# Five pairs of expert weight blocks are multiplied in plain fp32 instead of as a split pair; the ring of raw weight buffers is lengthened by four once

## The reference, cut to what matters

```python
top_vals, top_idx = lax.top_k(logits, TOP_K)
gates = ...                                  # softmax of the two, spread over 8 experts
for e in range(N_EXPERTS):
    out = out + gates[:, e:e + 1] * swiglu(t, w_gate[e], w_up[e], w_down[e])
# swiglu(t, g, u, d) = (silu(t @ g) * (t @ u)) @ d ;  g, u: 1024 x 1792, d: 1792 x 1024, all float32
```

## Time and profile before

| | us |
|---|---|
| median of 3 runs | 1148.93 (1148.74 to 1149.09) |
| the profiled execution | 1148.72 |
| its span in the profile | 1147.0 |
| PE busy | 1123.6 (98% of the span) |
| DVE busy | 875.3 (76%) |
| ACT busy | 754.1 (66%) |

### The profile page before, as it was taken

One profiled execution on the slowest core, in us unless ns is written; L12 is line 12 of the kernel. 1 busy time (PEld: TensorE's weight loads), 2 busy tenths in 40 slices (PEclk: granted clock), 3 DMA queues, 4 the chain that ended last, 5 costly groups with the idle time before them and its releaser, 6 DMA issues.

```text
span 1147.0 us, 15735 instructions
## 1 busy us (share of the span) xinstructions
PE 1123.6 (98%) x5566; PEld 946.4 (83%) x5566; DVE 875.3 (76%) x983; ACT 754.1 (66%) x941; POOL 35.1 (3%) x64
## 2 busy tenths in 40 slices
PE   9999999999999999999999999999999999999996
PEld 8888888888888888888888888887778887888874
DVE  6568676765554556468676779999999899999997
ACT  6555656455344345556656466799987898988785
POOL 3001000000000001001001000000000000000000
PEclk9999999999999999999999999999999999999999
DMA  9845533668555354646533657999999999999993
GB/s 322 278 141 183 175 99 98 210 207 311 183 181 187 110 173 144 217 133 186 172 101 125 198 178 249 405 396 406 407 407 394 371 398 403 405 407 406 407 384 128
DMA packets 120554, 294.96 MB, mean 257 GB/s; under 512 B 9006, under 2 KB 33676, under 8 KB 119964
## 3 DMA queue, kind: packets, MB, share of 16 engines
q1 hardware_dynamic: 119072, 288.23, 69.7%
q0 software_dynamic: 960, 5.28, 1.2%
q10 hardware_dynamic: 444, 0.47, 0.1%
HBM read 292.90 MB, written 1.05 MB: 256 GB/s over the span
## 4 chain that ended last, share of the span: by engine, by line
PE 79%; DVE 15%; DMA 3%; ACT 2%; issue 1%; SPq 0%; ACTq 0%; DVEq 0%
PE bank L1716 22%; PE bank L1717 21%; PE bank L1718 21%; DVE w_lo L1491 9%; DVE w_lo_more L1491 3%; PE bank L2130 2%; PE bank L2131 2%; PE bank L1932 2%; PE bank L1952 2%; PE bank L1760 2%; DMA raw<-in_moe_w_gate 1%; PE bank L1940 1%; DMA raw<-in_moe_w_down 1%; PE bank L2113 1%; ACT w_hi L941 1%
## 5 line engine op out<-in xcount | busy, mean ns | idle before, releaser
L1162 DVE TENSOR_TENSOR w_lo<-raw,w_hi 128x1024 fp32r<-128x1024 f32 (+4 forms) x141 | 240.1, 1708 | 144.2 <-ACT w_hi L721 143.7
L721 ACT ACTIVATE w_hi<-raw 128x1024 fp32r<-128x1024 f32 (+5 forms) x141 | 201.4, 1432 | 152.8 <-PE bank L1718 152.8
L1491 DVE TENSOR_TENSOR w_lo<-raw,w_hi 128x1792 fp32r<-128x1792 f32 (+3 forms) x148 | 287.2, 1971 | 10.8 <-ACT w_hi L941 10.0
L941 ACT ACTIVATE w_hi<-raw 128x1792 fp32r<-128x1792 f32 (+3 forms) x148 | 244.4, 1668 | 45.8 <-PE bank L1718 29.4
L1716 PE MATMUL bank<-w_hi,aT_hi 128*128 128x512 f32 (+1 forms) x592 | 235.1, 397 | 0.9 <-DVE aT_lo L1274 0.6
L1718 PE MATMUL bank<-w_hi,aT_lo 128*128 128x512 f32 (+1 forms) x592 | 230.0, 388 | 0.0
L1717 PE MATMUL bank<-w_lo,aT_hi 128*128 128x512 f32 (+1 forms) x592 | 229.5, 388 | 0.0
L1716 PEld LDWEIGHTS bank<-w_hi,aT_hi 128*128 128x128 f32 x592 | 111.3, 188 | 22.6 <-DVE w_lo L1284 1.4
L1718 PEld LDWEIGHTS bank<-w_hi,aT_lo 128*128 128x128 f32 x592 | 111.1, 188 | 22.8
L1717 PEld LDWEIGHTS bank<-w_lo,aT_hi 128*128 128x128 f32 x592 | 111.4, 188 | 20.3
L1491 DVE TENSOR_TENSOR w_lo_more<-raw,w_hi_more 128x1792 fp32r<-128x1792 f32 (+3 forms) x50 | 97.0, 1947 | 5.7 <-ACT w_hi_more L941 5.7
(11 more groups left out here) (326 smaller groups left out, 1806.6 us busy)
## 6 DMA issues: line engine op xcount, KB each, us to landing
raw<-in_moe_w_gate SPq DMA_DIRECT2D x128, 448.0 KB, 7.0
raw<-in_moe_w_up SPq DMA_DIRECT2D x128, 448.0 KB, 7.0
raw<-in_moe_w_down SPq DMA_DIRECT2D x112, 512.0 KB, 7.2
raw<-in_w_in SPq DMA_DIRECT2D x40, 768.0 KB, 4.5
raw<-in_dense_w_gate SPq DMA_DIRECT2D x22, 512.0 KB, 3.9
raw<-in_dense_w_up SPq DMA_DIRECT2D x22, 512.0 KB, 4.8
raw<-in_dense_w_down SPq DMA_DIRECT2D x11, 1024.0 KB, 4.9
raw<-in_w_in SPq DMA_DIRECT2D x20, 512.0 KB, 5.0
```

Of the source, the lines that this page charges most:

```text
L721: act.activation(dst, src, ACT.Copy).then_inc(hi_made[j], 1)
L941: act.activation(split_of(hi_slot, m), raw_of(i, n), ACT.Copy).then_inc(e_hi_made, 1)
L1162: dve.tensor_tensor(dst, src, high, ALU.subtract).then_inc(lo_made[j], 1)
L1491: dve.tensor_tensor(split_of(lo_slot, m), raw_of(i, n), split_of(hi_slot, m).bitcast(F32), ALU.subtract).then_inc(e_lo_made, 1)
```

## The change

In each even small step (k = 2, 4, 8, 10, 14) the pair of up granules n = 9 and 10 is no longer split. PE multiplies the raw float32 weights by the float32 view of the tokens, one matmul where there were two (the hi and the lo columns of the stationary operand stay as they are). ACT and DVE skip that pair. SP, before it loads into a raw slot that held such a granule, waits until PE has used it instead of until DVE has made its lo part. These pairs are granules 48 and 49, 94 and 95, 186 and 187, 232 and 233, 324 and 325.

Granules 52 to 55 (end of step 2) are loaded once into four other buffers, in `mixed` and `xs`, where the outputs of the first two experts come later. The ring of 12 raw slots goes on behind them as if they weren't there: granules 56 to 67 take over slots from 16 granules back instead of 12; from granule 68 on it is 12 again. ACT waits for DVE to have read these buffers before it writes the first outputs there. The final residual's buffers move with the ring (`H_SLOTS`).

```diff
+WHOLE = {SPLIT_OF[SEQ[r, k, KC + 2]] for r in range(ROUNDS) for k in SMALL_STEPS if k % 2 == 0}
...
+OUTSIDE = range(52, 56)
+
+def raw_slot_of(i):
+
+    if i in OUTSIDE:
+        return RAW_SLOTS + i - OUTSIDE[0]
+    return (i - (len(OUTSIDE) if i > OUTSIDE[-1] else 0) + RAW_SLOTS // 2) % RAW_SLOTS
...
-H_SLOTS = (2, 3, 4, 5)
+H_SLOTS = (10, 11, 0, 1)
...
 # SP, before each load
+                            if i in OUTSIDE:
+                                sp.wait_ge(logits_made, 1)
+                                sp.wait_ge(sq_act, 4)
+                                sp.wait_ge(sq_dve, 4)
+                            elif RAW_BEFORE[i] is None:
...
-                                sp.wait_ge(e_lo_made, SPLIT_OF[RAW_BEFORE[i]] + 1)
+                                if is_whole(RAW_BEFORE[i]):
+                                    sp.wait_ge(e_used, RAW_BEFORE[i] + 1)
+                                else:
+                                    sp.wait_ge(e_lo_made, splits_made(RAW_BEFORE[i]))
...
 # ACT and DVE
-                for m in sorted({SPLIT_OF[first], SPLIT_OF[first + 1]}):
+                for m in sorted({SPLIT_OF[first], SPLIT_OF[first + 1]} - WHOLE):
...
 # ACT, output_hi
+                if r == 0 and e < 2:
+                    act.wait_ge(e_lo_made, splits_made(OUTSIDE[2 * e + 1]))
...
 # PE, gate_up_granule
-                pe.wait_ge(e_lo_made, SPLIT_OF[i] + 1)
+                if is_whole(i):
+                    pe.wait_ge(*raw_arrival(i))
+                    for u in range(2):
+                        last = pe.matmul(bank[(B_GATE, B_UP)[n // KC][u]][:, 0:HN], xT[:, c, small_both(p, k % 4 // 2)].bitcast(F32),
+                                         raw_of(i)[:, 0, u * HN:(u + 1) * HN], start=c == 0, stop=c == KC - 1)
+                    last.then_inc(e_used, 1)
+                    return
+                pe.wait_ge(e_lo_made, splits_made(i))
```

More of the change, by code:

```diff
@@ L166, with is_whole, splits_made @@
 SPLIT_OF = {i + x: m for m, (i, n) in enumerate(SPLITS) for x in range(n)}
+WHOLE = {SPLIT_OF[SEQ[r, k, KC + 2]] for r in range(ROUNDS) for k in SMALL_STEPS if k % 2 == 0}
+MADE, made = [], 0
+for m in range(len(SPLITS)):
+    made += m not in WHOLE
+    MADE.append(made)
+def is_whole(i):
+    return SPLIT_OF[i] in WHOLE
+def splits_made(i):
+    return MADE[SPLIT_OF[i]]
 def slot_history(slots):
     return [i - slots if i >= slots else None for i in range(len(GRANULES))]
-H_SLOTS = (2, 3, 4, 5)
-def h_slots_read(r, slots):
-    return SPLIT_OF[max(i for i in range(PER_ROUND * r, PER_ROUND * (r + 1)) if (i + RAW_SLOTS // 2) % RAW_SLOTS in slots)] + 1
-RAW_BEFORE, W_BEFORE = slot_history(RAW_SLOTS), slot_history(W_SLOTS)
+OUTSIDE = range(52, 56)
[4 more added lines that the diff above has]
+H_SLOTS = (10, 11, 0, 1)
+def h_slots_read(r, slots):
+    return splits_made(max(i for i in range(PER_ROUND * r, PER_ROUND * (r + 1)) if raw_slot_of(i) in slots))
+W_BEFORE = slot_history(W_SLOTS)
+RAW_BEFORE, RAW_TURN, last_in = [], [], {}
+for i in range(len(GRANULES)):
+    RAW_BEFORE.append(last_in.get(raw_slot_of(i)))
+    RAW_TURN.append(1 if RAW_BEFORE[i] is None else RAW_TURN[RAW_BEFORE[i]] + 1)
+    last_in[raw_slot_of(i)] = i
 BETWEEN = {(STEPS - 1, 20): ("hidden", STEPS - 1, 0)}
@@ L239, in build_trunk @@
             [("raw", [P, 2, 3, SLOT])],
-            [("raw_pad", [P, H_SLOTS[0], SLOT_W]), ("h_hi", [P, NT, D], F32R), ("h_lo", [P, NT, D], F32R)])
+            [("raw_pad", [P, H_SLOTS[0], SLOT_W]), ("h_hi", [P, NT, D], F32R)],
+            [("h_lo", [P, NT, D], F32R)])
         w_hi = place("w_hi", [P, 3, SLOT], F32R)
@@ L354, in build_trunk @@
                              "x_hi_in", "x_lo_in", "selT_tr", "selT_in", "y_hi_made", "y_lo_made", "back_made"))
-        e_raw_in = [sem(f"e_raw_in{s}") for s in range(RAW_SLOTS)]
+        e_raw_in = [sem(f"e_raw_in{s}") for s in range(RAW_SLOTS + 1)]
         e_hi_made, e_lo_made, e_used, e_silu_made, e_hid_made, e_hid_tr, e_hT_hi_made, e_hT_lo_made = (sem(n) for n in (
@@ L442, in raw_of, with raw_arrival @@
         def raw_of(i, n=1):
-            at_slot = (i + RAW_SLOTS // 2) % RAW_SLOTS
-            return raw_slot[:, at_slot:at_slot + n, 0:granule_width(GRANULES[i][2])]
+            of, at_slot = raw_slot, raw_slot_of(i)
+            if i in OUTSIDE:
+                of, at_slot = (mixed, xs)[(i - OUTSIDE[0]) // 2], (i - OUTSIDE[0]) % 2
+            return of[:, at_slot:at_slot + n, 0:granule_width(GRANULES[i][2])]
+        def raw_arrival(i):
+            if i in OUTSIDE:
+                return e_raw_in[RAW_SLOTS], 16 * len(OUTSIDE)
+            return e_raw_in[raw_slot_of(i)], 16 * RAW_TURN[i]
         def split_of(slots, m):
@@ L610, in expert_loads @@
                                     experts_at[k // 2] = sp.value_load(order[0:1, at_rank:at_rank + 1], min_val=0, max_val=EXPERTS - 1)
-                            if RAW_BEFORE[i] is None:
-                                s = (i + RAW_SLOTS // 2) % RAW_SLOTS
+                            if i in OUTSIDE:
+                                sp.wait_ge(logits_made, 1)
+                                sp.wait_ge(sq_act, 4)
+                                sp.wait_ge(sq_dve, 4)
+                            elif RAW_BEFORE[i] is None:
+                                s = raw_slot_of(i)
                                 sp.wait_ge(lo_made[s % 6 // 2], MIX[1] + (BLK_MIX, BLK_MIX + 1)[s < RAW_SLOTS // 2] + 1)
                             else:
-                                sp.wait_ge(e_lo_made, SPLIT_OF[RAW_BEFORE[i]] + 1)
+                                if is_whole(RAW_BEFORE[i]):
+                                    sp.wait_ge(e_used, RAW_BEFORE[i] + 1)
+                                else:
+                                    sp.wait_ge(e_lo_made, splits_made(RAW_BEFORE[i]))
                             if n < GU_N:
@@ L621, in expert_loads @@
                                 src = moe_w_down[0][ds(experts_at[(k - 1) // 2], 1), row:row + P, :]
-                            sp.dma_start(raw_of(i)[:, 0, :], src.rearrange("o p n -> (o p) n")).then_inc(e_raw_in[i % RAW_SLOTS], 16)
+                            sp.dma_start(raw_of(i)[:, 0, :], src.rearrange("o p n -> (o p) n")).then_inc(raw_arrival(i)[0], 16)
                     expert_loads(0)
@@ L931, in expert_hi @@
             def expert_hi(first):
-                for m in sorted({SPLIT_OF[first], SPLIT_OF[first + 1]}):
+                for m in sorted({SPLIT_OF[first], SPLIT_OF[first + 1]} - WHOLE):
                     i, n = SPLITS[m]
                     for x in range(i, i + n):
-                        act.wait_ge(e_raw_in[x % RAW_SLOTS], 16 * (x // RAW_SLOTS + 1))
+                        act.wait_ge(*raw_arrival(x))
                     if W_BEFORE[i] is None:
@@ L1487, in expert_lo @@
             def expert_lo(first):
-                for m in sorted({SPLIT_OF[first], SPLIT_OF[first + 1]}):
+                for m in sorted({SPLIT_OF[first], SPLIT_OF[first + 1]} - WHOLE):
                     i, n = SPLITS[m]
-                    dve.wait_ge(e_hi_made, m + 1)
+                    dve.wait_ge(e_hi_made, MADE[m])
                     dve.tensor_tensor(split_of(lo_slot, m), raw_of(i, n), split_of(hi_slot, m).bitcast(F32),
```

## The result

The changed kernel takes 1155.36 us (median of 6 runs, 1154.45 to 1156.73) against 1148.84 us for the kernel before in the same sessions: a ratio of 1.0058, 95% interval 1.0048 to 1.0068, or 6.5 us slower. The forecast was 1153.8 us, slower by 5.1, with a range of 1148.5 to 1157.5; the measured time is inside it, 1.6 us above the forecast.

The account below looks back on a forecast made before the run. PE and DVE were taken to bound alternate stretches, with loads close behind. Steps 2, 4, 8, 10 and 14 added 1.4 + 0 + 0.9 + 1.4 + 1.4 = 5.1 us to 1148.72: 1153.8 us, range 1148.5 to 1157.5.

Parts of the forecast that it names:

- PE's price of an unsplit pair: PE's added work for each unsplit pair of granules: 1.44 us, 7.2 us over five pairs.
- rival 3: An unsplit matmul takes only the 0.41 us of the two it replaces, so PE pays nothing: 1144.2 us, chance 0.03.
- Steps 2, 10 and 14: PE's time is added in 2 and 14; in 10 the late silu leaves DVE idle: +1.4 us each.
- Step 8: PE's time is added, less about 0.5 us of its wait for a hidden lo part: +0.9 us.
- Step 4: Where DVE leads, PE's delay and DVE's relief cancel: 0, bounds -2.0 and +1.4 us.
- DVE's relief: Lo parts no longer made, 2.02 us a pair: hidden in PE's stretches, turned into idle wait in step 10.
- Rivals 1, 2: DVE's relief counts: in steps 4 and 10, 1148.4 us, chance 0.10; in step 14 too, 1145.0 us, chance 0.11.
- Rival 5: PE's gaps soak up the shift of steps 2 and 8, leaving 2.8 us: 1151.5 us, chance 0.12.
- SP's new wait: Raw slots of unsplit granules held until PE's use, longest in step 14: 0 on the path, other end +3 us.
- The four extra slots: Four loads go early, but PE leads there: 0, bound -1.1 us.
- rival 4: Loads starve as well; DMA idling of steps 10 and 14 lands on the path: +3, 1156.8 us, chance 0.12.

Follow-up runs that it names:

- experiment 3: Changed kernel with all pairs split, old SP waits; PE repeats the ten granules' products on 400 of 448 columns: 1153.52 us, 1.0043 against the kernel before.
- Experiment 5: Changed kernel, pairs multiplied from old hi and lo slots in PE's old time, ACT and DVE skipping them: 1151.79 us; also without SP's wait for PE: 1148.78.
- experiment 6: Changed kernel with the unsplit pair moved behind the gate rows' addition: 1156.62 us; the same move made to experiment 3: 1152.76 us.
- experiment 4: Changed kernel with all pairs split, SP still waiting for PE's use: 1151.34 us; holding only step 10's pair 1150.00, only step 14's 1149.76.

## Why the prediction was right

- **PE's price of an unsplit pair**, from attention's fp32 product: forecast 1.44 us, measured 1.37. Right. A matmul of 448 columns takes 2 x 0.376 = 0.75 us against 0.205 for one fp32r product, 3.7 times. That agrees with the four passes on the Trainium skill's page FP8 and Floating Point Precision, section TensorE Precision Notes. The half rate of rival 3, read as the cost of the whole matmul, would have given 0.41 and is excluded; each of the two records runs at nearly half rate.
- **Steps 2, 10 and 14**: +1.4, +1.45 and +1.4 in the chain, as forecast. Other traces with longer pairs agree: the kernel without extra slots and that of experiment 3 have +1.3 and +1.4 in step 10 and +1.4 and +1.45 in step 14.
- **Step 8**: +0.9, the right number with another cause. The forecast took 0.5 off because DVE's skipped work would shorten PE's wait for a hidden lo part. Experiment 3 skips nothing, and its trace shifts by 0.94 in the same place (901.94 to 903.61, 937.63 to 940.24); there too PE no longer waits for `hT_lo_buf`. PE itself comes later.
- **Step 4**: open. The chain shows 0.0 by the landmark at 824, but +0.8 by 852.34 (854.54), and the kernel without extra slots shows +1.3 and +1.05. The kernel with the slots alone gains 0.8 by 852 as well, with nothing changed in step 4. The forecast's balance of delay and relief has no support, as the relief alone measures nothing.
- **DVE's relief counts for nothing in the sum**: right, and more firmly so than argued. The forecast had it swallowed by the late silu in step 10, and let it cancel PE's delay in step 4. Experiment 5 shows it at 0, to within 1 us, even when no silu is late, and the traces of experiment 6 that the silu is one of two gates. Rivals 1, 2 and 3 are all out, and rival 3 by a second reason: with PE's cost and the held slots taken away the kernel stands at 1148.8, not 1144.2. Rival 5 is out as well: the shift of step 2 is not soaked up by PE's gaps (1.39 at 770, 1.40 at 824), nor is that of step 8.
- **The sum of PE's steps is right in part by luck.** The unsplit pairs add 5 x 1.37 = 6.9 us of PE work. Experiment 3 adds 7.3 us and measures +5.0. The forecast took a similar 2.1 us off, 7.2 to 5.1, but mostly on the strength of DVE's relief in steps 4 and 8, and experiment 3 has no relief. Its trace gives up the difference in step 4, in step 8 and behind step 14, where its shift falls by 1.2 us.
- **The step that was mis-sized is SP's new wait.** The forecast took it as 0 "on the path, since ACT reaches these granules late as well" and kept +3 as the other end. Alone, with the extra slots in the kernel, it measures +2.8 (1.0013 to 1.0031, 1.5 to 3.6 us), +2.1 against the slots alone. The reason given does not quite hold at the granules themselves, where ACT waits 0.29 us for the late load, and it left out what comes behind them: experiment 4 has loads on the chain 20 to 40 us later, where DVE has caught up with them. How the cost divides among the five steps is open: +1.2 for step 10 and +1.0 for step 14 both hold the slots' own +0.7.
- **The four extra slots**: 0, as forecast, within an interval of about 1 us each way.
- **The sum.** PE's time (+5.0) and held slots (+2.8) make 7.8, or 7.1 with the slots' +0.7 counted once; the whole change is 6.5. With intervals of about 1 us each way, that is near enough to say that these two are the cost, and not near enough to say whether they overlap. The +0.8 and +1.2 between the steps of the chain lie in or next to stretches where the kernel with the slots alone shifts by 1.1 and 0.75 in one trace. That the held slots add to the second is likely, from experiment 4, and open for the first.

The truth lies halfway between the forecast and rival 4, which priced this wait at +3.

## What to carry to other kernels

Here four resources were all within a few per cent of the bound. Some 7 us of work added to PE cost 5.0 us (experiment 3), and the work taken from ACT and DVE returned nothing. In such a kernel, check a relief by removing the work with nothing put in its place before you count on it. Before a buffer is freed by a later reader than before, compare the delay with what is queued at the DMA engines, and don't put what is not covered at nothing if loads run at their full rate behind it: it can appear tens of microseconds downstream. A shift read from a single trace has to be held against the trace of a kernel with no reason to shift, and a part of the change that stays in every experiment, as the extra slots here, needs a run of its own as their control.

## What the runs showed of the hardware

- A matmul of 448 columns with plain fp32 on both sides is two records that start 0.376 us apart, 0.75 us in all, against 0.205 us for one fp32r product: 3.7 times. Attention's narrower ones had already shown 1.72 ns a column; here it is 1.68.
- With twelve slots for granules of 448 to 512 KB, the load rate levels at 404 to 409 GB/s for tens of microseconds. A stop of SP of 5.0 us cost 1.7 us of loading, and in the 30 us behind it no rate above 409 made up for it.
- Ten granules less to split (10 us of DVE's time) changed the run time by 0.0%, in an interval of 0.09% each way.
